# Split-operand products in stick-breaking attention: scores and softplus sums as products of high and low parts

## The reference

```python
z = einsum('bqhd,bshd->bhqs', q, k) * (SB_HEAD_DIM ** -0.5)
log_beta = log_sigmoid(z)
log_keep = where(causal, log_beta - z, 0.0)              # = -softplus(z)
rest = cumsum(log_keep, axis=3, reverse=True) - log_keep # sums over later keys
w = where(causal, exp(log_beta + rest), 0.0)
out = einsum('bhqs,bshd->bqhd', w, v)
```

## Time and profile before

| | us |
|---|---|
| median of 3 executions | 529.55 (528.54 to 532.43) |
| the profiled execution, its span | 529.8 |
| PE busy | 448.5 (85%) |
| DVE busy | 291.5 (55%) |
| ACT busy | 241.3 (46%) |
| POOL busy | 194.1 (37%) |
| attention, from the first prompt head's scores (173.87) to the output projection (248.91) | 75.0 |

### The profile page before, as it was taken

One profiled execution on the slowest core, in us unless ns is written; L12 is line 12 of the kernel. 1 busy time (PEld: TensorE's weight loads), 2 busy tenths in 40 slices (PEclk: granted clock), 3 DMA queues, 4 the chain that ended last, 5 costly groups with the idle time before them and its releaser, 6 DMA issues. The chain is left out here.

```text
span 529.8 us, 7155 instructions
## 1 busy us (share of the span) xinstructions
PE 448.5 (85%) x2569; PEld 333.4 (63%) x2569; DVE 291.5 (55%) x411; ACT 241.3 (46%) x330; POOL 194.1 (37%) x189
## 2 busy tenths in 40 slices
PE   1899999998979899999999961689999999999300
PEld 1677887777758576656777861466766766666200
DVE  2626332443243446565150747269898898998136
ACT  4625121343333536456113531167787777876100
POOL 3442100474540000001000761266767767746261
PEclk9999999998979999999999986599999999999855
DMA  8547202222331300000297397359999999993267
GB/s 300 165 72 280 62 24 81 83 77 80 119 125 56 109 1 1 1 1 1 90 390 275 128 354 242 91 191 338 342 348 330 331 344 316 362 366 131 85 228 277
DMA packets 61700, 95.31 MB, mean 180 GB/s; under 512 B 9265, under 2 KB 42033, under 8 KB 61665
## 3 DMA queue, kind: packets, MB, share of 16 engines
q1 hardware_dynamic: 47040, 69.48, 38.7%
q0 software_dynamic: 5088, 17.89, 10.4%
q10 hardware_dynamic: 9536, 7.50, 4.3%
HBM read 81.82 MB, written 13.04 MB: 179 GB/s over the span
## 5 line engine op out<-in xcount | busy, mean ns | idle before, releaser
L1272 DVE TENSOR_TENSOR wlo<-raw,whi 128x2048 fp32r<-128x2048 f32 (+1 forms) x45 | 96.9, 2154 | 24.4 <-ACT whi L866 24.4
L1384 PE MATMUL bank<-whi,xT_hi 128*128 128x512 f32 x224 | 93.6, 418 | 2.5 <-issue 1.9
L1385 PE MATMUL bank<-wlo,xT_hi 128*128 128x512 f32 x224 | 90.8, 405 | 0.0
L1386 PE MATMUL bank<-whi,xT_lo 128*128 128x512 f32 x224 | 90.8, 405 | 0.0
L866 ACT ACTIVATE whi<-raw 128x2048 fp32r<-128x2048 f32 x45 | 86.0, 1912 | 6.2 <-PE bank L1386 6.2
L591 POOL TENSOR_TENSOR wlo<-raw,whi 128x1024 fp32r<-128x1024 f32 x16 | 59.6, 3724 | 34.4 <-ACT whi L866 34.4
L953 DVE TENSOR_TENSOR wlo<-raw,whi 128x2048 fp32r<-128x2048 f32 x14 | 32.0, 2287 | 52.6 <-ACT whi L657 52.6
L1384 PE MATMUL bank<-whi,xsT_hi 128*96 128x512 f32 x128 | 53.4, 417 | 4.4 <-DVE xsT_lo L1278 3.1
L1384 PEld LDWEIGHTS bank<-whi,xT_hi 128*128 128x128 f32 x224 | 43.6, 195 | 14.6 <-issue 4.2
L1386 PE MATMUL bank<-whi,xsT_lo 128*96 128x512 f32 x128 | 51.4, 402 | 0.0
L1385 PE MATMUL bank<-wlo,xsT_hi 128*96 128x512 f32 x128 | 51.3, 401 | 0.0
(11 more groups left out here) (214 smaller groups left out, 773.2 us busy)
## 6 DMA issues: line engine op xcount, KB each, us to landing
raw<-in_w_gate_dram SPq DMA_DIRECT2D x32, 512.0 KB, 6.3
raw<-in_w_up_dram SPq DMA_DIRECT2D x32, 512.0 KB, 7.8
raw<-in_w_down_dram SPq DMA_DIRECT2D x32, 512.0 KB, 7.2
raw<-in_w_in_dram SPq DMA_DIRECT2D x10, 1024.0 KB, 5.4
expert_rows<-yout POOLq DMA_DIRECT2D x16, 384.0 KB
raw<-in_w_out_dram SPq DMA_DIRECT2D x4, 1024.0 KB, 5.1
x_sb<-in_x_prompt_dram SPq DMA_DIRECT2D x4, 512.0 KB, 8.8
normed_tokens<-xn ACTq DMA_DIRECT2D x4, 512.0 KB, 2.7
```

The lines of the kernel that those rows point to most:

```text
L1272: dve.tensor_tensor(wlo[SPLIT_OF[m3]][:, 0:n], eraw[slot][:, 0:n], whi[SPLIT_OF[m3]][:, 0:n].bitcast(F32), ALU.subtract).then_inc(m_lo, 1)
L1384: pe.matmul(acc, x_hi, w_hi, start=start, stop=False)
L1385: pe.matmul(acc, x_hi, w_lo, start=False, stop=False)
L1386: return pe.matmul(acc, x_lo, w_hi, start=False, stop=stop)
```

## The change

Scores: `q_two` holds per head the high part of q in the head's 64 partitions and its low part in the other 64; `k_hi2` holds the high part of k twice. One float32r product over 128 partitions then gives high times high and low times high, and a second one, over 64 partitions, adds low k times high q. Sums: softplus is written in place over the logarithms, DVE casts it to a float32r high part, and the low part is a subtraction, on POOL for the first three quarters and on DVE for the rest; PE runs the sums for each part with two matrices of -1 in float32r, straight over the chunks, without the added-up chunks of before. Within a head the banks are now taken in the order 1, 2, 0 ("tail", 768 columns, then "head", 512 columns). The low parts of q and k are taken by DVE (`qk_lo`), behind the copies of ACT; for k ACT makes four copies of 64 partitions in place of one of 128. To make room, two of the `raw` buffers and `whi[1]`, `wlo[1]` serve the attention, so that the first two softplus passes wait for the end of the input projection, and units 11 and 12 are loaded only when the attention's last product with v is done (unit 13 behind three loads of experts); their splits move behind the attention.

```diff
@@ -122,33 +123,39 @@
         mix = ExitStack()
         xT_hi = sb("xT_hi", [P, KC, SEQ], F32R, stack=mix)
         xT_lo = sb("xT_lo", [P, KC, SEQ], F32R, stack=mix)
-        qpad = sb("qpad", [P, HEADS, SEQ], stack=mix)
+        q_two = sb("q_two", [P, HEADS, SEQ], F32R, stack=mix)
...
-        lw = [sb(f"lw{i}", [P, ZW], stack=st_b)[:, :] for i in range(3)]
+        lw = [sb("lw0", [P, ZW], stack=st_b)[:, :], raw[2][:, 0:ZW], raw[0][:, 0:ZW]]
 
         lw += [x_[:, :, :].rearrange("p c n -> p (c n)")[:, 0:ZW] for x_ in (ckT, cv)]
-        sp = [sb(f"sp{i}", [P, ZW], stack=st_b) for i in range(2)]
-        later = sb("later", [P, 6 * P], stack=st_b)
+        s_hi = [whi[1][:, 0:ZW], s_hi1[:, :]]
+        s_lo = [wlo[1][:, 0:ZW], s_lo1[:, :]]
+        k_lo = sb("k_lo", [P, KCH, SEQ], F32R, stack=st_b)
+        k_hi2 = sb("k_hi2", [P, HEADS, SEQ], F32R, stack=st_b)
         st_b.close()
...
@@ -274,10 +282,10 @@
                 return [bank[5], bank[6], bank[7]]
             return [bank[0], bank[1], bank[2]] if h % 2 else [bank[3], bank[4], bank[7]]
 
-        regions = [(0, 0, 512, 0, 0), (1, 0, 384, 1, 128), (1, 384, 128, 3, 384), (2, 0, 256, 2, 256)]
...
@@ -339,6 +350,8 @@
             def load_unit(n):
                 if n >= 3:
                     unit_used(sp_, n - 3)
+                if U_IN < n < U_IN + 3:
+                    sp_.wait_ge(pv_ok, NV)
...
-            for n in range(2, U_ALL):
+            for n in range(2, U_ALL - 1):
                 load_unit(n)
...
                 for m in range(NRAW):
+                    if isinstance(r, int) and m == 3:
+                        load_unit(U_ALL - 1)
                     first(m)
...
+            for h in range(NH):
+                pool.wait_ge(s_hi_ok, 2 * h + 1)
+                for p, c in stored_parts(h, 0):
+                    ins = pool.tensor_tensor(s_lo[h % 2][0:p, c], lw[h % 5][0:p, c], s_hi[h % 2][0:p, c].bitcast(F32), ALU.subtract)
+                ins.then_inc(s_lo_tail, 1)
...
@@ -720,21 +743,27 @@
                         act.wait_ge(qk_tr, m + 1)
                         src = turn_bank(QK_USE + m)[:, :].rearrange("p (j n) -> p j n", j=KCH)[:, :, 0:rows[t]]
                         if name == "v":
-                            act.activation(kT[:, :, tok(t)], src, ACT.Copy).then_inc(qkT_ok, 1)
+                            if t < NT - 1:
+                                k4 = k_hi2[:, :, :].rearrange("p (j a) n -> p j a n", a=2)
+                                act.activation(k4[0:HD, :, 0, tok(t)], src[0:HD], ACT.Copy)
+                                act.activation(k4[HD:P, :, 1, tok(t)], src[HD:P], ACT.Copy)
+                                act.activation(k4[HD:P, :, 0, tok(t)], src[0:HD], ACT.Copy)
+                                act.activation(k4[0:HD, :, 1, tok(t)], src[HD:P], ACT.Copy).then_inc(qk_hi, 1)
+                            else:
+                                act.activation(kT_s[:, :, :], src, ACT.Copy).then_inc(qk_hi, 1)
                             dst = k_prompt[0, 0, tok(t)] if t < NT - 1 else k_sample[0, 0]
                             act.dma_start(dst.rearrange("t h d -> t (h d)"), qn[m % 2][0:rows[t], :]).then_inc(k_out[m % 2], 16)
...
-                                q4 = qpad[:, :, :].rearrange("p (j a) n -> p j a n", a=2)
+                                q4 = q_two[:, :, :].rearrange("p (j a) n -> p j a n", a=2)
                                 act.activation(q4[0:HD, :, 0, tok(t)], src[0:HD], ACT.Copy)
-                                act.activation(q4[HD:P, :, 1, tok(t)], src[HD:P], ACT.Copy).then_inc(qkT_ok, 1)
+                                act.activation(q4[HD:P, :, 1, tok(t)], src[HD:P], ACT.Copy).then_inc(qk_hi, 1)
...
             def weights(h):
-                act.wait_ge(sp_ok, h + 1)
...
                 if h + 1 < NH:
                     exp_log(h + 1)
                 weights(h)
-                if h == 7:
-                    split_hi(U_IN + 1)
                 if h >= 5 and h % 2:
...
+            split_hi(U_IN + 1)
             split_hi(U_IN + 2)
...
@@ -1005,35 +1036,42 @@
 
                 if h >= 2:
                     dve.wait_ge(rest_ok, 2 * (h - 1))
-                s, u = sp[h % 2], later_sums(h)
-                if h == 0:
-                    link(dve.memset(s[:, 1024:ZW], 0.0))
+                else:
+                    dve.wait_ge(proj_done, NT * NB)
+                b_, hi, lo = lw[h % 5], s_hi[h % 2], s_lo[h % 2]
                 for a in range(2):
                     dve.wait_ge(l_ok, 2 * h + a + 1)
                     for bk, p, c in parts_of(h, a):
-                        ins = dve.scalar_tensor_tensor(out=s[0:p, c], in0=z_of(h)[bk][0:p, 0:c.stop - c.start], scalar=0.0,
-                                                       in1=lw[h % 5][0:p, c], op0=ALU.max, op1=ALU.add)
-                ins.then_inc(sp_ok, 1)
-                dve.wait_ge(sp_ok, h + 1)
...
-                for k, a, b in adds:
-                    ins = dve.tensor_tensor(u[:, k * n:(k + 1) * n], a, b, ALU.add)
-                    if k:
-                        link(ins)
-                ins.then_inc(later_ok, 1)
+                        ins = dve.scalar_tensor_tensor(out=b_[0:p, c], in0=z_of(h)[bk][0:p, 0:c.stop - c.start], scalar=0.0,
+                                                       in1=b_[0:p, c], op0=ALU.max, op1=ALU.add)
+                    ins.then_inc(sp_ok, 1)
+                    dve.wait_ge(sp_ok, 2 * h + a + 1)
+                    for p, c in stored_parts(h, a):
+                        ins = dve.tensor_copy(hi[0:p, c], b_[0:p, c])
+                    ins.then_inc(s_hi_ok, 1)
+                dve.wait_ge(s_hi_ok, 2 * h + 2)
+                dve.tensor_tensor(lo[:, 0:512], b_[:, 0:512], hi[:, 0:512].bitcast(F32), ALU.subtract).then_inc(s_lo_head, 1)
+
+
+            def qk_lo(m):
+                t, two = m % NT, (q_two, k_hi2)[m // NT]
+                dve.wait_ge(qk_hi, m + 1)
+                if t == NT - 1:
+                    dve.sem_inc(qkT_ok, 1)
+                    return
+                src = turn_bank(QK_USE + m)[:, :].rearrange("p (j n) -> p j n", j=KCH)
+                t4 = two[:, :, :].rearrange("p (j a) n -> p j a n", a=2)
+                for a in range(2):
+                    own, other = (slice(HD * x, HD * (x + 1)) for x in (a, 1 - a))
+                    dst = k_lo[own, :, tok(t)] if m >= NT else t4[other, :, a, tok(t)]
+                    ins = dve.tensor_tensor(dst, src[own], t4[own, :, a, tok(t)].bitcast(F32), ALU.subtract)
+                ins.then_inc(qkT_ok, 1)
 
 
             for b, name in enumerate(BLOCKS):
+                if name in ("k", "v"):
+                    for t in range(NT - 2, NT):
+                        qk_lo(NT * (name == "v") + t)
                 split_lo(2 * b + 2)
...
                         dve.tensor_reduce(ssq8[0:p, m, :], sqt[m % 2][0:p, :].rearrange("p (h d) -> p h d", h=HEADS), AX.X,
                                           ALU.add).then_inc(ssq8_ok, 1)
                         dve.wait_ge(rstd8_ok, m + 1)
+                        if t >= 2:
+                            qk_lo(m - 2)
                         if m >= 2:
...
@@ -1111,14 +1151,13 @@
                     softplus(h + 1)
                 if h == 1:
                     sb_lo(0)
-                if h == 7:
-                    split_lo(U_IN + 1)
...
                 if h:
+                    hd = h - 1
+                    own = slice(HD * (hd % 2), HD * (hd % 2 + 1))
                     for bk, c0, n, c, q0 in regions:
-                        if h >= 2 and c == 1:
+                        if h >= 2 and bk == 0:
                             pe.wait_ge(w_ok, 2 * (h - 2) + 2)
-                        pe.matmul(z[bk][:, c0:c0 + n], kT[:, (h - 1) // 2, c * P:(c + 1) * P], qpad[:, h - 1, q0:SEQ],
-                                  start=(c0 == 0), stop=True, skip_group_check=True)
+                        kc, zz = slice(c * P, (c + 1) * P), z[bk][:, c0:c0 + n]
+                        pe.matmul(zz, k_hi2[:, hd, kc], q_two[:, hd, q0:SEQ], start=(c0 == 0), stop=True, skip_group_check=True)
+                        pe.matmul(zz, k_lo[own, hd // 2, kc], q_two[own, hd, q0:SEQ], start=False, stop=True,
+                                  skip_group_check=True)
                         mm = pe.matmul(z[bk][:, c0:c0 + P], identb[:, :], maskneg[:, :], start=False, stop=True,
                                        skip_group_check=True)
-                        if bk == 0:
+                        if bk == 2:
                             mm.then_inc(z_ok, 1)
...
             def suffix_sums(h):
 
-                z, s = z_of(h), sp[h % 2]
-                pe.wait_ge(sp_ok, h + 1)
+                z = z_of(h)
+                place = {c: (bk, c0, n, q0) for bk, c0, n, c, q0 in (regions if h else s_regions)}
+
+                def sums_of(c, s):
+
+                    bk, c0, n, q0 = place[c]
+                    for c2 in range(c, len(place)):
```

(39 more changed lines are left out.)

94 lines of the change are left out of this document (47 added, 47 removed).

## The result

The changed kernel took 552.74 us (median of 4 runs, 549.9 to 553.89) beside 529.35 for the kernel before: ratio 1.0399, 95% interval 1.0354 to 1.0445. A second set of runs gave 1.0430 (1.0385 to 1.0474). I had predicted 535.0 in a range of 530 to 541: slower was right, the size was not. The profiled execution has a span of 552.3 us against 529.8. An execution's time is some 1.6 us more than its span (553.89 for the span of 552.3), so the span of 529.8, from which the sum was counted up, was not of one kind with the median beside it; that is small against the miss.

A forecast was written before the change was run, and what follows sets the result against it. PE was taken to bound the attention, POOL and DVE the chains of q and k, where PE waits. 529.8 + 9.4 (q and k) + 1 (clock) - 5.1 (attention) = 535.1, predicted as 535.0 us, range 530 to 541.

The forecast's parts named there:

- q and k: Chains of q and k: low parts on DVE ahead of the scaling cost 5.0 us for q, 4.4 for k.
- the rival that it is hidden anyway: Chains of q and k: low parts fit into DVE's wait for POOL's root; 529.8 us, not slower; chance 0.12.
- The attention's start: Ahead of head 3: cheaper scores and sums on PE give back 2.5 us, less 0.4 of waiting: gain 2.1.
- the clock: PE's granted clock falling to the 1.2 GHz level after more waits: between nothing and 2 us, taken as 1.
- The fourth rival: Attention: the clock falls, three heads at twice 4.95 us, or unit 11 is late; 538 to 545 us; chance 0.12.
- The first rival: Attention gives nothing: casts at the subtraction's price or narrow products at 0.23 us; gain 0.5 to 1, time 539; chance 0.22.
- The head's chain: DVE and ACT per head: 6.6 us (6.0 to 7.3), casts 0.56 and 0.43; DVE's chain becomes the bound.
- POOL's low part: Heads: POOL's subtraction of 768 columns, 1.7 to 2.8 us, costed at nothing except up to 1 after the last head.
- the five periods: Heads 3 to 8: five at 6.6 us plus 0.65 make 33.65 instead of 36.6, gain 3.0.
- Scores on PE: Per head on PE: scores 1.4 us instead of 2.65, with sums at 2.3 instead of 3.63.
- the signs that I had named for being wrong: Head period 7.3 or more, or 5; v's second half under 6 us after 153.80; PE at 0.50 in heads.
- Weights: Output projection: loading and splitting unit 11 takes 9.7 us, hidden within 11; unit 12 has 11 more; cost nothing.

The follow-up runs named there:

- first experiment: Changed kernel with 18 products of 256 columns that nobody reads filling TensorE's two waits between the transposes of the gated block: 551.57 us, ratio 1.0398.
- run with four repairs: Changed kernel with q/k low parts behind the scaling, k's low part on 128 partitions, head's high part from PSUM, sample's sums in fp32: 540.27 us, ratio 1.0177.
- second mended version: Run with four repairs, plus the head's low-part subtraction behind the next head's absolute values and the sample's softplus early: 533.15 us, ratio 1.0025.

## Why the prediction was wrong

**q and k: right, and in size.** q's chain is 5.2 us longer (predicted 5.0), k's 4.35 (predicted 4.4). The reason was the one given, the low part in the order ahead of the scaling; the run with it behind the scaling gave 7.9 us back, and the rival that it is hidden anyway falls. Only the store of k is issued beside the first copy, not behind the fourth, so that k's late tile waits for the copies (6.46 us for ScalarE's k_hi), not for the store.

**The attention's start, the main step that failed: the clock, and a term left out.** The start was to gain 2.1 us and cost 10.4. These 12.5 us are most of the 17 that the sum is short. By the marks 6.0 of the 10.4 lie in sums(0), 2.0 in scores(2), 0.8 in sums(1), 0.6 ahead of sums(0), and 1.0 in the absolute values of head 3, which now wait for 768 columns of scores instead of 512.

For the clock I wrote "Between nothing and 2 I take 1". It cost about 7 here, at the place where I had read that PE was busy 2.46 of 4 us and kept 1.00. The 7 are an estimate: scores(2) took 4.65 us and sums(1) 4.38 at 0.50, where heads at 1.00 take 2.83 and 2.89; five products of sums(0) took 2.25 us at 0.50 and 1.36 at 1.00 (first experiment), so that sums(0) would take some 6.4 to 7 instead of 10.6.

The rest has nothing to do with the clock, as the run with sums(0) in fp32 shows: at 1.00 the start is still 5.6 us longer than before (14 fp32 products in its sums(0), 8.2 us). My sum had no term for sums(0), which became 28 float32r products and one in fp32, where nine in fp32 took 4.6 us; by the estimate above it is dearer at full clock too. And 1.25 us were to come back from scores(2), which are no cheaper than before.

The fourth rival had the clock falling in the attention, at a chance of 0.12, in three heads with PE waiting. It did fall there twice, for some 4 us each, but for 17 us ahead of them, with PE busy. The first rival, that the attention gives nothing, named narrow products at 0.23 us each, which is near what sums(0) cost at full clock by the estimate (28 in about 6 us); its slow casts did not come true.

The profiled executions of the changed kernel and its variants tell more of the clock in the start. With the waits and float32r sums(0) it fell in all seven; with the waits filled and float32r sums(0) it fell (the first experiment); with the waits and fp32 sums(0) it held once and fell three times; with the waits filled and fp32 sums(0) it held in all three. So the waits and the short float32r products both seem to matter, and to take away one is not enough; this rests on one execution of each kernel, and on a single one with filled waits and float32r sums. Before it fell the engine had run products of 256 columns 0.2 to 0.3 us apart, or waited and transposed. Why either lets it fall, and why the kernel before kept it over the same waits, stays open.

The Trainium skill (TensorE: Matmul & The Clock Gate, HAM oscillation — how this bites in real kernels) puts a fall of the clock down to gaps in which the engine idles. The first experiment disagrees, by the busy time that the profile shows: from 188 to 192 PE was busy 4.00 of 4.00 us, and the clock fell at 191. The measurement decides.

**The head's chain: the casts were right, their cover was not.** Without GpSimd the casts take the 0.56 and 0.43 us that I took. The step that failed is "POOL's low part ... I cost it at nothing". It is hidden from PE, but VectorE's next cast cannot run beside it: 1.54 - 0.43 = 1.1 a head, and 6.6 + 1.1 = 7.7 is the measured period. So the five periods cost 2.4 us instead of gaining 3.0. Both directions were shown: VectorE's cast or subtraction in SBUF waits for GpSimd, and GpSimd waits for VectorE's subtraction; an operand in PSUM lifts it.

The Trainium skill (SBUF — State Buffer, Who interferes with whom) states this as a rule: VectorE's fast two-port modes, and its instructions with two SBUF inputs, contend with GpSimd for one pair of ports, and the later one blocks for the whole instruction. The runs agree (0.43 against 1.54, 0.69 against 1.21, 1.81 against 2.34); I had not weighed it.

**Scores on PE: mis-sized.** I had 1.4 us a head and it is 2.83, because of the turns between 128 and 64 partitions; on 128 alone 1.79. Sums have 2.89 where I had 2.3. Nothing of this reached the period of the heads, which VectorE set, as the sum assumed; at the start, which PE sets, it did.

Of the signs that I had named for being wrong two came: a period above 7.3, though not for the reason given there, since the casts were sized rightly, and PE at 0.50 in the heads.

**Weights: right.** Unit 11 was rounded and split from 274.92 to 279.16, while unit 12's rounding waited until 282.05 for PE to finish the first half of the output projection; no wait of PE there.

```profile
274.92 1.92 ACT L680 ACTIVATE whi<-raw 128x2048 fp32r<-128x2048 f32 x1 [4.48 <-DMA raw<-in_w_out_dram]
...
282.05 1.92 ACT L680 ACTIVATE whi<-raw 128x2048 fp32r<-128x2048 f32 x1 [5.21 <-PE bank L1445]
```

**The range** took the unknown prices at their bounds, one at a time. The clock, which I had put at 1, and GpSimd's neighbour and sums(0), which I had put at nothing, were out of it, and they came together.

## What to carry to other kernels

Cheaper products on the bounding engine can cost it its clock: price the lower level wherever they come to stand beside waits, and if it falls, try removing the waits and the short products together. Price every pass of the loop, the odd first one too, by the number of its products. Work given to GpSimd is not free for VectorE: check which of VectorE's instructions beside it read only SBUF, and place them before, after, or with an operand in PSUM. A low part that is issued where the engine's order puts it in the loop from tile to tile costs its whole length; issue it where the engine waits anyway, as the subtraction behind the next head's absolute values (period 7.25 in the run with four repairs, 5.98 in the second mended version, both with scores on 128 partitions).
